# Attention's input projection spread over the convolution's norm and over retention's tiles, with the residual H kept in DRAM meanwhile

## What is computed

```
p_lat = u_lat @ w_in_l
kA_l, vA_l, kB_l, vB_l, qA_l, qB_l, gF_l, gB_l, pool_l, glu_l = _split_cols(p_lat)
qA = _apply_rope(_heads_qk(qA_l), *rope_a)                 # differential attention
yA_lat = _diff_head_out(_diff_attn_blocks(qA, kA_all, vA_all, lam), g_subln_l, lam_init)
yf = _retention(qB, kB, vB, s_cf)[0]                        # chunkwise retention, both ways
yC_lat = _pool_mixer(pool_l, w_pool_l, s_pool_l)
yD_lat = _conformer_conv(glu_l, ...)                        # h = _layer_norm(conv(h)); silu(h) @ w_pw2
y_lat = jnp.concatenate([yA_lat, yB_lat, yC_lat, yD_lat], axis=-1) @ w_out_l
h_lat = h_lat + gm * _rms_norm(y_lat, g_post_mix[l])        # H, the residual
```

## Time and profile before

| | us |
|---|---|
| median of three runs | 3371.68 |
| the profiled execution's own time | 3365.28 |
| its span in the profile | 3362.7 |
| granted TensorE clock, mean | 0.924 of full speed |

### The profile page before, as it was taken

One profiled execution on the slowest core, in us unless ns is written; L12 is line 12 of the kernel. 1 busy time (PEld: TensorE's weight loads), 2 busy tenths in 40 slices (PEclk: granted clock), 3 DMA queues, 4 the chain that ended last, 5 costly groups with the idle time before them and its releaser, 6 DMA issues.

```text
span 3362.7 us, 46590 instructions
## 1 busy us (share of the span) xinstructions
PE 2931.6 (87%) x17578; PEld 1647.2 (49%) x17578; DVE 2009.5 (60%) x2788; ACT 1198.9 (36%) x2040; POOL 577.6 (17%) x434
## 2 busy tenths in 40 slices
PE   5798789777989999999997579689778899999997
PEld 2454554454545656757754234454554343444443
DVE  4883755787356413635645695656883575164765
ACT  5111214676344322313334311314774443232332
POOL 0500010000223501202212230010001234030221
PEclk8899769799999999999998789769998999999998
DMA  5110012111224321111131111012222242111133
GB/s 214 42 43 19 7 41 68 45 58 42 76 71 162 125 88 47 48 51 39 51 138 38 62 38 38 7 42 71 81 81 70 75 154 90 38 63 50 63 117 121
DMA packets 65855, 233.16 MB, mean 69 GB/s; under 512 B 8864, under 2 KB 9632, under 8 KB 65696
## 3 DMA queue, kind: packets, MB, share of 16 engines
q1 hardware_dynamic: 64544, 225.71, 20.2%
q10 hardware_dynamic: 1152, 5.24, 0.4%
HBM read 211.26 MB, written 14.68 MB: 67 GB/s over the span
## 4 chain that ended last, share of the span: by engine, by line
PE 55%; issue 23%; DVE 15%; ACT 5%; POOL 1%; DMA 1%; SPq 0%; DVEq 0%; POOLq 0%; ACTq 0%
PE PS L707 34%; PE PS L812 17%; DVE R L2018 4%; DVE wlo L1680 2%; ACT X L1330 1%; ACT R L1328 1%; DVE R L1842 1%; DVE R L1829 1%; ACT whi L1213 1%; DMA R<-in_w_ada 1%; POOL st L2400 1%; PE PS L1026 1%; DVE R L2140 1%; PE PS L741 1%; DVE X L2114 1%
## 5 line engine op out<-in xcount | busy, mean ns | idle before, releaser
L707 PE MATMUL PS<-R,whi 128*128 128x512 f16 (+1 forms) x5568 | 1522.2, 361 | 101.8 <-DVE wlo L1680 58.1
L707 PE MATMUL PS<-R,wlo 128*128 128x512 f16 (+1 forms) x2784 | 1003.0, 360 | 0.0
L707 PEld LDWEIGHTS PS<-R,whi 128*128 128x128 f16 x5568 | 544.1, 99 | 669.0 <-issue 73.9
L1680 DVE SCALAR_TENSOR_TENSOR wlo<-stage,whi 128x1024 f16<-128x1024 f32 (+1 forms) x204 | 278.8, 1367 | 399.6 <-ACT whi L1213 385.5
L812 PE MATMUL PS<-R,whi 128*128 128x256 f16 (+2 forms) x2352 | 510.2, 326 | 0.0
L707 PEld LDWEIGHTS PS<-R,wlo 128*128 128x128 f16 x2784 | 275.3, 99 | 272.6 <-issue 15.8
L812 PE MATMUL PS<-R,wlo 128*128 128x256 f16 (+2 forms) x1176 | 319.2, 326 | 0.0
L812 PEld LDWEIGHTS PS<-R,whi 128*128 128x128 f16 x2352 | 230.2, 98 | 151.9
L1213 ACT ACTIVATE whi<-stage 128x1024 f16<-128x1024 f32 (+1 forms) x204 | 210.4, 1031 | 138.8 <-PE PS L707 85.0
L2018 DVE SCALAR_TENSOR_TENSOR R<-X,small,R 128x1024 f32<-128x1024 f32 (+1 forms) x180 | 219.0, 1263 | 1.8
L2332 POOL TENSOR_TENSOR X<-X 128x512 f32<-128x512 f32 (+1 forms) x98 | 135.6, 1387 | 452.0 <-ACT X L1584 332.3
(11 more groups left out here) (222 smaller groups left out, 3318.2 us busy)
## 6 DMA issues: line engine op xcount, KB each, us to landing
stage<-in_w_gu SPq DMA_DIRECT2D x120, 512.0 KB, 3.7
X<-in_w_ada SPq DMA_DIRECT2D x60, 512.0 KB, 3.3
stage<-in_w_down SPq DMA_DIRECT2D x48, 512.0 KB, 3.4
stage<-in_w_in SPq DMA_DIRECT2D x44, 512.0 KB, 3.3
stage<-in_w_out SPq DMA_DIRECT2D x32, 512.0 KB, 3.3
T<-in_w_ada SPq DMA_DIRECT2D x20, 512.0 KB, 3.4
h_save<-R SPq DMA_DIRECT2D x16, 640.0 KB, 5.4
R<-h_save SPq DMA_DIRECT2D x16, 640.0 KB, 4.8
```

The source lines that it names most:

```text
L707: last = mm(slot(j, t0, t1)[:, c0 - t0:c1 - t0], w[:, j, k, :], row, start=(k == 0 and q == 0), stop=(k == K - 1 and q == 2))
L1680: STT(wlo[:, j, 0:K, :], stage[:, j, 0:K, :], WS, whi[:, j, 0:K, :], ALU.mult, ALU.subtract).then_inc(S["w_lo"], 1)
```

## The change

- **Units 16 and 17 (attention's keys)** are issued on PE inside the norm stage: 16 between the mean product and the variance product, 17 behind the variance product and two pooling products. Both write PSUM's second slot (`into=1`), the norm's sums both the first. Their evictions, weight halves and the pooling's are placed accordingly on ACT and DVE.
- **Units 18 to 21** are cut in chunks of up to 512 columns and in k-steps; `a_turns` spreads the steps over three turns per tile of the tile loop: behind the product with the states, behind the masked product, and behind the next tile's scores. The chunks use PSUM banks 6 and 7 in turn; ACT evicts each.
- **Rows.** Attention's rows now lie in H..H+5, swapped rows in H+6, H+7, U, U+1. So H leaves SBUF: in layer 0 it is simply loaded again from the input x, in layer 1 its eight rows are written to DRAM (`h_save`) beside the first weight loads; in both layers one row is loaded back per round of the modulation's loads during attention, and the output projection's second half waits for `h_back`.
- **Behind the loop**: the transposes of the values come first. The rotation is software-pipelined: POOL multiplies by the cosine (a new instruction there), DVE multiplies the swapped row by the sine and adds; the low half of a chunk is made one chunk later; the stacks' copies go three to ACT and one to DVE, two chunks later.

```diff
+        def a_turns(l):
+            n = TILE_TURNS * (NTILE - first_tok(l) // P)
+            steps = [(c, k, c1 - c0) for c, (_, c0, c1, _, _) in enumerate(a_chunks(l)) for k in range(KD)]
+            total, cum, turns = sum(w for _, _, w in steps), 0, [[] for _ in range(n)]
+            for c, k, w in steps:
+                turns[min(n - 1, cum * n // total)].append((c, k))
+                cum += w
+            return turns
...
+                    stream(unit0(l, "in") + 2, KD, KD, a["w_in"][l][2:2 + KD], lambda r, j: sp.dma_start(
+                        h_save[bass.ds(2 * r + j, 1)].rearrange("a p t -> p (a t)"),
+                        R[:, bass.ds(2 * r + (H + j), 1), :].rearrange("p a t -> p (a t)")).then_inc(S["h_saved"], 16))
...
+                    sp.dma_start(R[:, bass.ds(r + H, 1), :].rearrange("p a t -> p (a t)"),
+                                 h_from[bass.ds(r, 1)].rearrange("a p t -> p (a t)")).then_inc(S["h_back"], 16)
...
                 last.then_inc(S["mean_ps"], 1)
-                pool_products(0, 2)
+                pe.wait_ge(S["slot_free"], u0 + 16)
+                gemm_unit(u0 + 16, 0, KD, U, 0, into=1)
                 pe.wait_ge(S["cd_sq"], at("cd_sq", l) + 2)
...
                 last.then_inc(S["var_ps"], 1)
-                pool_products(2, 2 * len(sp0))
+                pe.wait_ge(S["pooled"], at("pooled", l) + 2)
+                pe.wait_ge(S["roped"], at("roped", l) + len(rope_chunks(l)))
+                pool_products(0, 2)
+                pe.wait_ge(S["slot_free"], u0 + 17)
+                gemm_unit(u0 + 17, 1, KD, U, 0, into=1)
+                pool_products(2, 4)
...
+                def a_turn(x):
+                    for c, k in turns[x]:
+                        v, c0, c1, first, end = chunks[c]
+                        if k == 0 and first:
+                            pe.wait_ge(S["w_lo"], u0 + v + 1)
+                        if k == 0 and c >= 2:
+                            chunk_gone(c - 2)
+                        for q, (w, part) in enumerate(((whi, 0), (whi, 1), (wlo, 0))):
+                            last = mm(PS[:, 6 + c % 2, 0:c1 - c0], w[:, v % 2, k, :], hl(U + k, part, c0, c1),
+                                      start=(k == 0 and q == 0), stop=(k == KD - 1 and q == 2))
+                        if k == KD - 1:
+                            last.then_inc(S["units" if end else "a_ps"], 1)
...
                 for t in range(tq, NTILE):
                     retained_out(t)
+                    a_turn(TILE_TURNS * (t - tq) + 1)
                     if t > tq:
                         turned_out(t - tq - 1)
                     if t < NTILE - 1:
                         inner_scores(t + 1)
+                    a_turn(TILE_TURNS * (t - tq) + 2)
...
-                pe.wait_ge(S["yb_sum"], at("yb_sum", l) + NTILE - tq)
-                for u in range(A_UNITS):
-                    gemm_unit(u0 + 16 + u, u % 2, KD, U, 0 if u < 2 or u >= 4 else t0)
...
+                        own.link(TT(swapped[:, c0:c1], swapped[:, c0:c1], xrow(3)[:, c0:c1], ALU.mult))
+                        dve.wait_ge(S["cosed"], at("cosed", l) + m + 1)
...
+                        TT(sum_half(m), row[:, c0:c1], swapped[:, c0:c1], ALU.add).then_inc(S["rot"], 1)
...
+                for i, c0, c1 in rotary(l):
+                    pool.wait_ge(S["swapped"], at("swapped", l) + 16 * (i + 1) * (P // 16))
+                    TT(arow(i)[:, c0:c1], arow(i)[:, c0:c1], xrow(2)[:, c0:c1], ALU.mult).then_inc(S["cosed"], 1)
```

More of the change, by code:

```diff
@@ L272, in arow, with swap_row, a_units, a_chunks @@
         def arow(i):
-            return (R[:, Y + i, :], xrow(i - 2), R[:, U + i - 4, :])[i // 2]
+            return R[:, H + i, :]
         def arow16(i, c0, c1):
-            return R16[:, Y + i, c0:c1] if i < 2 else X16[:, 2 * PADW * (i - 2) + c0:2 * PADW * (i - 2) + c1]
+            return R16[:, H + i, c0:c1]
+        def swap_row(i):
+            return R[:, (H + 6, H + 7, U, U + 1)[i], :]
+        TILE_TURNS = 3
+        def a_units(l):
+            return [(v, 0 if v >= 20 else first_tok(l)) for v in (18, 19, 20, 21)]
+        def a_chunks(l):
+            return [(v, c0, c1, c0 == tr, c1 == TOK) for v, tr in a_units(l) for c0, c1 in spans(tr)]
+        def a_turns(l):
[6 more added lines that the diff above has]
+            return turns
+        def a_done(l):
+            return {c: x for x, turn in enumerate(a_turns(l)) for c, k in turn if k == KD - 1}
+        def a_inner(l, c):
+            return sum(not last for _, _, _, _, last in a_chunks(l)[:c])
+        def a_out_at(l, n, turn):
+            end = lambda n, turn: TILE_TURNS * n + (2 * turn - 1)
+            before = end(n, 0) if turn else end(n - 1, 1)
+            return [c for c, x in sorted(a_done(l).items()) if before < x <= end(n, turn)]
+        def a_tile(l, v):
+            c = next(c for c, (w, _, _, _, last) in enumerate(a_chunks(l)) if w == v and last)
+            return next(n for n in range(NTILE + 1) for turn in range(2) if c in a_out_at(l, n, turn))
+        def stacked(n):
+            return n // 4 if n % 4 == 3 else n - n // 4
         def rope_chunks(l):
@@ L706, in products @@
                         row = hl(row0 + k, part, c0, c1) if half_of is None else half_row(row0 + k, part, c0, c1, half_of)
-                        last = mm(slot(j, t0, t1)[:, c0 - t0:c1 - t0], w[:, j, k, :], row,
+                        last = mm(slot(into, t0, t1)[:, c0 - t0:c1 - t0], w[:, j, k, :], row,
                                   start=(k == 0 and q == 0), stop=(k == K - 1 and q == 2))
@@ L1080, in inner_scores, with chunk_gone @@
                     last.then_inc(S["sc_ps"], 1)
+                turns, chunks = a_turns(l), a_chunks(l)
+                def chunk_gone(c):
+                    v, _, _, _, last = chunks[c]
+                    if last:
+                        pe.wait_ge(S["slot_free"], u0 + v + 1)
+                    else:
+                        pe.wait_ge(S["a_out"], at("a_out", l) + a_inner(l, c) + 1)
+                def a_turn(x):
[10 more added lines that the diff above has]
+                            last.then_inc(S["units" if end else "a_ps"], 1)
                 def retained_out(t):
@@ L1484, in pool_hi, with a_row @@
                           scale=sm(l, "s_pool", j)).then_inc(S["pool_hi"], 1)
-                pool_hi(0, 2)
+                def a_row(v, into):
+                    act.wait_ge(S["units"], u0 + v + 1)
+                    tr = 0 if v < 18 else t0
+                    A(arow(v - 16)[:, tr:TOK], slot(into, tr), ACT.Copy, scale=UNS * XS).then_inc(S["slot_free"], 1)
+                hi_part(u0 + 17, 1, KD)
                 for j in range(2):
@@ L1489, in _ @@
                     A(xrow(j)[:, t0:], R[:, Y + 6 + j, t0:], ACT.Square).then_inc(S["cd_sq"], 1)
+                if l:
+                    act.wait_ge(S["h_saved"], 16 * KD * 2 * l)
+                a_row(16, 1)
+                hi_part(u0 + 18, 0, KD)
                 act.wait_ge(S["var_ps"], at("var_ps", l) + 1)
-                A(xrow(2)[:, t0:], slot(1, t0), ACT.Sqrt, scale=1.0 / 256, bias=epsv[:, 1:2]).then_inc(S["ln_root"], 1)
-                pool_hi(2, 4)
+                A(xrow(2)[:, t0:], slot(0, t0), ACT.Sqrt, scale=1.0 / 256, bias=epsv[:, 1:2]).then_inc(S["ln_root"], 1)
+                pool_hi(0, 2)
+                a_row(17, 1)
                 for j in range(2):
@@ L1533, in gated_hi, with a_chunk_out @@
                       scale=XS * 0.5 * UNS).then_inc(S["yb_hi"], 1)
+                def a_chunk_out(c):
+                    v, c0, c1, _, end = a_chunks(l)[c]
+                    if end:
+                        act.wait_ge(S["units"], u0 + v + 1)
+                    else:
+                        act.wait_ge(S["a_ps"], at("a_ps", l) + a_inner(l, c) + 1)
+                    A(arow(v - 16)[:, c0:c1], PS[:, 6 + c % 2, 0:c1 - c0], ACT.Copy, scale=UNS * XS
+                      ).then_inc(S["slot_free" if end else "a_out"], 1)
+                    if end and v < 21:
+                        hi_part(u0 + v + 2, v % 2, KD)
                 for n in range(NTILE - tq):
+                    for c in a_out_at(l, n, 0):
+                        a_chunk_out(c)
                     if n >= 2:
```

178 lines of the change are left out of this document (102 added, 76 removed).

## The result

The changed kernel took 3284.55 us (median of four executions, 3283.33 to 3287.1), the kernel before on the same chip 3372.09: ratio 0.9745, 95% interval 0.9732 to 0.9757, 87.5 us less. The forecast was 3296 us, 75.6 us less.

What follows compares the result with a forecast made beforehand. PE was busy 87% of the span, so stages mattered only where it waits or runs at half clock; DVE paced the tile loop. +2 + 8 + 11 + 13 - 57 - 52.6 = -75.6 us on 3371.68 gave 3296 us, range 3272 to 3320.

Steps and rivals of the forecast that it cites:

- Unit 16 thus costs nothing: Norm stage, layer 0: PE's idle time and faster clock cover unit 16's 13.0 us; reciprocal at 331.6 instead of 332.51.
- The place named as late next: Norm stage, layer 0: tanh stands behind unit 17's eviction on ACT, so the pointwise product starts at 351.3, 2 us late.
- PE's own pieces: Tile loop: PE's work per tile without the turns, 7.24 us at 1.2 GHz, scaled to 3.95 us at full clock.
- the breaks between types: Tile loop: six breaks between f16 and f32 products add 0.3 us a tile, bounds 0 and 1.5.
- the sign of being right: Tile loop: 9.2 to 10.3 us between states' products, with granted clock above 0.9 in both loops.
- The reason for the clock: Tile loop: full clock, as the f16 projection stream fills over half of PE's time and the scan ahead is at 1.00.
- The rival at 1.2 GHz: Tile loop: clock stays at half, PE needs 17.6 and 18.9 us a tile, +91 and +84, 3447 us; chance 0.06.
- The rival of turns that don't hide: Tile loop: each turn adds to DVE's cycle, loops grow by 98.6 us instead of 24, about 3371 us; chance 0.07.
- the argument on the first two turns: Tile loop: the first (1.7 us) hides behind DVE's masks (1.28 us), the second before transposes waiting for POOL's power.
- DVE's loss to POOL: Behind the loop: DVE loses 0.67 us per microsecond of POOL's multiplications, 8.6 and 7.7 us, bounds 0 and 15.
- The chain rival: Rotation: DVE waits for POOL, ACT and PE in turn, wide chunk 4.6 us instead of 3.4, 3336 us; chance 0.13.
- The whole exclusion of POOL and DVE: Rotation: DVE loses all POOL's time, 12.8 and 11.5 us instead of 8.6 and 7.7, 3304 us; chance 0.10.

Runs made afterwards that it cites:

- e1: Changed kernel with units 16 and 17 moved out of the norm stage, in line behind the pointwise product; 3311.63 us, ratio to before 0.9832.
- e11: Changed kernel with the mean's product waiting again for key rotation, pooling and unit 15's slot, units 16 and 17 staying in the norm stage; 3295.35 us.
- e5: Changed kernel with ACT's two tanh before unit 17's eviction and DVE's products behind them before unit 18's weight half; ratio to before 0.9724.
- e12: e2 with four f32 products a tile, whose result nobody reads, in the turns' three places in the loop; 3343.5 us, ratio to before 0.9929.
- e2: Changed kernel with the turns of units 18 to 21 moved out of the tile loop, in one piece behind it; 3348.41 us, ratio to before 0.9934.
- e8: Changed kernel with each tile's turns in one piece at the last of the three places; 3290.84 us, ratio to before 0.9761.
- e3: Changed kernel with the rotation's cosine multiplications back from POOL on DVE; 3289.36 us, ratio to before 0.9763.
- e4: Changed kernel with each new H transfer moving 16 of its 1280 columns, so its result is wrong; 3286.39 us, ratio to before 0.9759.

## Why the prediction was right, point by point

**Norm stage.** +2 and +8 us predicted, +3.1 and +10.7 measured, within the bounds. Counted from PE's release for the mean, the reciprocals came as forecast (in layer 0 0.7 us earlier than before for 0.9, in layer 1 5.9 us later for 5.9), and so did the starts of the pointwise product (351.94 for 351.3; 11.1 us later for 11.2). Mis-sized was that product's length, forecast at full clock, 3.2 and 3.3 us shorter than before; it was 1.3 and 0.4 us shorter. PE had been idle for 4.59 and 4.38 us ahead of it, and its first part in each layer stands so (columns as in the earlier trace rows):

```profile
351.94:357.00 5.06, 5.06 (x8) 2.20 (x9) 1.69 (x3) 0.66 (x2) 0.35 (x2) 0.66 0.35 56
```

```profile
2094.56:2099.00 4.44, 4.44 (x6) 1.84 (x7) 1.41 (x2) 1.19 (x3) 0.35 (x2) 0.50 0.25 38
```

Granted clock 0.66 and 0.50. In layer 1 this is the whole miss; in layer 0 the pooling pair with its eviction and low half lies on the chain too (362.50 to 365.27), 1.9 us more between the product and the scan for the 1.3 forecast, against which the forecast held about 2 us for DVE's weight halves.

"Unit 16 thus costs nothing" holds only against the kernel before. Against e1, where the mean is as early but no unit stands between the sums, the reciprocals come 5.8 and 9.3 us later; by the estimate from e1 both units cost the stage 10.4 and 15.5 us, and the early mean, which the change could have had without them, paid 7.7 and 2.9 of it (e11, with the units in place). I had put both into one sum and so had not seen the units' part as a loss. The place named as late next, the tanh behind unit 17's eviction, is where e5 found 4.6 and 7.3 us.

**Tile loop.** +11 and +13 predicted, +6.5 and +8.4 measured. The step was right (PE becomes the bound, the turns hide between the waits, full clock), the size off by two terms: PE's own pieces, 3.95 us by scaling with the masked product's 2.00/3.67, are 0.65 + 1.73 + 0.53 + 0.65 = 3.6 us from start to start (the lengths that I had scaled overlap at their ends, as 1.90 us long and 1.73 to the next shows); and 8.87 - 3.56 - 5.2 leaves 0.1 us for the breaks between types, not 0.3. So the tile came out at 8.87 us, below the 9.2 to 10.3 that the prediction named as the sign of being right. The reason for the clock was too narrow: I took the f16 stream for what holds it, and e12 held it with f32 products. The rival at 1.2 GHz is refuted for this much work, and e2 shows that its premise was real: without the turns the loop stands at 0.50. The rival of turns that don't hide is refuted by e2: 13.2 us paid for 98.6. That the places matter (e8, 9 us over both loops) is what the argument on the first two turns rested on.

**Behind the loop.** -57 and -52.6 predicted, -55.9 and -52.4 measured. The terms came out one by one: the tables' wait 7.9 and 7.6 us for 6.4 and 6.8, DVE's own work 26.1 and 23.1 for 26.8 and 23.8 (e3's busy time less the cosine), DVE's loss to POOL 8.3 and 7.3 for 8.6 and 7.7, and what is left, filling, draining and DVE's waits for PE's stacks (2.02 us in the row at 513.24, then 0.55 to 0.94), 5.3 and 5.2 for 4.7. The loss to POOL has some luck in it: POOL's own time was 14.8 and 13.2 us for 12.8 and 11.5, and DVE lost 0.56 and 0.55 us for each of them, not 0.67. The chain rival (a wide chunk at 4.6 us) comes near only beside POOL: three chunks, one of them narrow, took 12.5 us there (494.97 to 507.49) and 7.3 us later (513.85 to 521.13). The whole exclusion of POOL and DVE, which the Trainium skill states ("SBUF — State Buffer", Who interferes with whom), would give 14.8 us of DVE time lost in layer 0; DVE lost 8.3, so here the rule holds in kind and not in size.

**H.** Hidden, as predicted (e4).

The sum of the errors: +1.1 + 2.7 in the norm stages, -4.5 - 4.6 in the loops, +1.1 + 0.2 behind: -4.0 us on a sum of -75.6. The rest up to -87.5 is 1.5 us of span outside these stages, 0.9 around the span, and 5.6 for the distance of the two profiled executions from their medians.

## What to carry to other kernels

An engine that is idle between others' steps is cover, but price each moved piece against the best version without it, not only against the kernel before: here an earlier start in the same edit paid for a part of the cost. Where a move lands work in front of a small instruction that others wait for (the tanh behind an eviction), look at that queue's order next; and a table that is loaded behind a loop can often go into what the loop has finished reading. A loop at half clock, as this one was, may take on work for nothing, and the busy share on the page does not tell how much room it has. And a few microseconds in which PE waits cost more than their own length when the sums behind them start at the lower clock, as the pointwise product did.

## What the runs showed of the hardware that was not expected

Work that nobody needs cost nothing: four f32 products a tile, 3.8 us at full clock, took layer 0's loop of e2 from granted clock 0.50 to 0.98, and the loop was no longer (B -0.9 and -0.4 us). A third of the f16 stream gave 0.85 and 0.89 in the two loops. A wait of 4.78 us ahead of short sums cost three more by the clock (e11), and PE's idle 4.59 and 4.38 us ahead of the pointwise product cost 1.7 and 2.8 (e5). And twelve multiplications on POOL, 14.8 us beside DVE, cost DVE 8.3 us, more than the 6.4 that it needs to do them itself, while its copy out of PSUM in the midst of them kept its 0.69 us.
